# Attention in a two-layer encoder: the transposed softmax weights' 64-row rests of two head groups in one PSUM bank, copied by ScalarE

## The reference, cut to what matters

```python
# 16 query heads, 2 key/value heads of width 64; chunks of 64 frames, window = own chunk + 1 before
scores = einsum("bcqkgd,bcskd->bckgqs", q, k_band) * (HEAD_DIM ** -0.5)
scores = where(valid, scores + bias, NEG_INF)          # bias = -slope[head] * distance
m = maximum(max(scores, axis=-1), sink)
p = exp(scores - m)
denom = sum(p, axis=-1) + exp(sink - m)
o = einsum("bckgqs,bcskd->bcqkgd", p / denom, v_band)
```

## Time and profile before

| | |
|---|---|
| three timed runs | 2421.97, 2423.84, 2426.55 us; median 2423.84 |
| the profiled execution | 2419.16 us, its span 2417.4 us |
| TensorE busy over the span | 2330.7 us (96%) |
| VectorE, ScalarE, GpSimd busy | 1433.3, 793.6, 410.1 us |
| mean granted TensorE clock | 0.987 of full speed |
| attention's rounds | about 1515 to 1649 us of the span |

### The profile page before, as it was taken

One profiled execution on the slowest core, in us unless ns is written; L12 is line 12 of the kernel. 1 busy time (PEld: TensorE's weight loads), 2 busy tenths in 40 slices (PEclk: granted clock), 3 DMA queues, 4 the chain that ended last, 5 costly groups with the idle time before them and its releaser, 6 DMA issues.

```text
span 2417.4 us, 41380 instructions
## 1 busy us (share of the span) xinstructions
PE 2330.7 (96%) x16362; PEld 1900.6 (79%) x16362; DVE 1433.3 (59%) x1994; ACT 793.6 (33%) x1265; POOL 410.1 (17%) x401
## 2 busy tenths in 40 slices
PE   7999989998999999999999999788999999999999
PEld 6888878787778888888888788446788888888887
DVE  4444567775337656755665733873275676567655
ACT  5011234444123322332233423662143233223323
POOL 0000011111322110211121400432311111102110
PEclk9999999999999999999999999998999999999999
DMA  3231100002111111112111110001111111111112
GB/s 126 77 137 57 47 3 4 4 3 98 58 38 53 49 56 52 45 51 61 52 43 52 56 44 27 1 0 44 35 44 54 59 44 51 52 60 44 52 53 88
DMA packets 167185, 119.29 MB, mean 49 GB/s; under 512 B 3663, under 2 KB 164261, under 8 KB 166565
## 3 DMA queue, kind: packets, MB, share of 16 engines
q1 hardware_dynamic: 164284, 100.65, 14.0%
q0 software_dynamic: 2736, 17.04, 1.9%
q10 hardware_dynamic: 56, 0.01, 0.0%
HBM read 106.68 MB, written 10.49 MB: 48 GB/s over the span
## 4 chain that ended last, share of the span: by engine, by line
PE 93%; DVE 5%; issue 1%; ACT 1%; DMA 0%; SPq 0%; DVEq 0%; ACTq 0%
PE ps L280 36%; PE ps L385 25%; PE ps L378 14%; PE ps L1157 2%; PE ps L1179 1%; PE ps L1926 1%; PE ps L2278 1%; PE ps L334 1%; DVE probs L1955 1%; DVE softmax_stats L1960 1%; PE ps L1211 1%; PE ps L1895 1%; PE ps L1690 1%; PE ps L1188 1%; DVE probs_t_b L2009 1%
## 5 line engine op out<-in xcount | busy, mean ns | idle before, releaser
L235 ACT CAST w_hi<-w_raw 128x1024 fp32r<-128x1024 f32 x180 | 189.3, 1052 | 818.1 <-PE ps L280 597.4
L280 PE MATMUL ps<-h_hi,w_hi 128*128 128x512 f32 x1264 | 395.6, 394 | 10.0 <-DVE h_lo L587 6.3
L744 DVE TENSOR_TENSOR residual<-residual,ps 128x512 f32<-128x512 f32 x448 | 299.5, 685 | 159.7 <-PE ps L385 155.8
L280 PE MATMUL ps<-h_lo,w_hi 128*128 128x512 f32 x1264 | 391.5, 391 | 0.0
L280 PE MATMUL ps<-h_hi,w_lo 128*128 128x512 f32 x1264 | 391.5, 391 | 0.0
L280 PEld LDWEIGHTS ps<-h_hi,w_hi 128*128 128x128 f32 x1264 | 236.3, 189 | 60.8 <-issue 10.7
L280 PEld LDWEIGHTS ps<-h_lo,w_hi 128*128 128x128 f32 x1264 | 238.6, 189 | 50.4
L280 PEld LDWEIGHTS ps<-h_hi,w_lo 128*128 128x128 f32 x1264 | 238.6, 189 | 50.2
L239 DVE TENSOR_TENSOR w_lo<-w_raw,w_hi 128x1024 fp32r<-128x1024 f32 x180 | 224.5, 1247 | 25.5 <-ACT w_hi L235 25.5
L712 POOL TENSOR_TENSOR w_sums_raw<-w_raw 128x256 f32<-128x256 f32 x64 | 52.9, 826 | 1079.6 <-DMA w_raw<-in_mlp_down 660.3
L378 PE MATMUL ps<-h_lo,w_hi 128*128 128x512 f32 x512 | 199.2, 389 | 0.0
(11 more groups left out here) (383 smaller groups left out, 3957.3 us busy)
## 6 DMA issues: line engine op xcount, KB each, us to landing
w_raw<-in_mlp_up SPq DMA_DIRECT2D x64, 512.0 KB, 4.0
w_raw<-in_mlp_down SPq DMA_DIRECT2D x64, 512.0 KB, 3.3
w_raw<-in_w_in_ab SPq DMA_DIRECT2D x26, 512.0 KB, 3.8
w_raw<-in_w_qkv SPq DMA_DIRECT2D x10, 512.0 KB, 3.9
x_in_tile<-in_x POOLq DMA_DIRECT2D x8, 512.0 KB, 7.1
x_spill<-residual POOLq DMA_DIRECT2D x1, 4096.0 KB, 12.6
w_raw<-in_w_out_ab SPq DMA_DIRECT2D x8, 512.0 KB, 3.7
w_raw<-in_w_o SPq DMA_DIRECT2D x8, 512.0 KB, 3.8
```

Of the source, the lines that this page charges most:

```text
L235: nc.scalar.copy(WH[:, slot], WR[:, slot]).then_inc(w_hi, 1)
L280: m = nc.tensor.matmul(acc(a_slot, half), ww, xx[:, k, half * HALF:(half + 1) * HALF], start=first, stop=last)
L744: dn_dve.done(TT(xk, xk, PS[:, bank_n, :], ALU.add), step)
```

## The change

The 64-row rests of the values and of the softmax weights are kept in halves of the partitions. The b parts of two groups go to the two halves of bank 5, that of the odd group into rows 64 to 127 by a matmul against the identity in place of a transpose, and ScalarE copies the bank once for both (`r0` behind group 1, `r1` behind group 3). VectorE no longer copies rests. The a parts use banks 4, 6, 7 and 4 for groups 0 to 3. The values exist in a second, shifted token-major form `VREST`, whose 64 rows stand in both halves, made by 8 more transposes and 8 matmuls at the start and copied by ScalarE. The value products go group by group: for each group and each par one product with the 128-row part and one with the 64-row rest, each with 256 moving columns (two heads); output bank 6 takes the even groups and bank 7 the odd ones. They wait for copies group by group.

```diff
-    VTOK = at("v_token_major", [9, P], 190.5)
+    VTOK = at("v_token_major", [NT, P], 190.5)
+    VREST = at("v_rest_twice", [NT, P], 198.5)
-    PTB = at("probs_t_b", [NQ, P], 82)
+    PTB = at("probs_t_b", [NKV, 4, P], 82)
+        def turned(dst, src, half):
+            if half:
+                return nc.tensor.matmul(dst, src, ident, start=True, stop=True)
+            return nc.tensor.transpose(dst, src, ident)
         def v_transposes(t):
...
-            for n in range(9):
-                m = nc.tensor.transpose(bank((6, 7, 5)[n // 4])[:, n % 4], VP[:, P * n:P * n + P], ident)
+            for n in range(NT):
+                m = nc.tensor.transpose(bank(6 + n // 4)[:, n % 4], VP[:, P * n:P * n + P], ident)
+            m.then_inc(v_tr, 1)
+            for n in range(NT):
+                for half in two:
+                    m = turned(bank(4 + n // 4)[half_rows(half), n % 4], VP[:, P * n + P:P * n + P + RH], half)
             m.then_inc(v_tr, 1)
+        def v_rest_act(act):
+            act.wait_ge(v_tr, 2)
+            for n in two:
+                nc.scalar.copy(VREST[:, 4 * n:4 * n + 4], bank(4 + n)).then_inc(v_rest, 1)
...
-            nc.gpsimd.memset(PTB[RH:P], 0.0).then_inc(ptb_zero, 1)
...
-            v_pool.done(nc.gpsimd.tensor_copy(VST[:, s], VTOK[:, bass.ds(tile, 2), :]), "v")
+            for n, (v, step) in enumerate(((VTOK, "own"), (VREST, "rest"))):
+                v_pool.done(nc.gpsimd.tensor_copy(VST[:, s, n], v[:, bass.ds(tile, 1), :]...), step)
...
+        TA_BANK = (4, 6, 7, 4)
         def probs_transposes(t, tile, s, g):
...
-            if g > 0:
-                pv_act.wait(t, tile, f"e{g - 1}")
-                pv_dve.wait(t, tile, f"e{g - 1}")
+            if g == 3:
+                pv_act.wait(t, tile, "e0")
+            elif at_start(tile, 1):
+                t.wait_ge(v_rest, 2)
+            else:
+                pv_act.wait(t, tile - 1, ("r1", "o0", "o1")[g])
+            if g == 2:
+                pv_act.wait(t, tile, "r0")
...
-                m = nc.tensor.transpose(bank(5)[0:RH, j], probs(tile, s, g)[:, j, P:WIN], ident)
+                m = turned(bank(5)[half_rows(g % 2), j], probs(tile, s, g)[:, j, P:WIN], g % 2)
         def value_products(t, tile, s):
...
+            for g in range(4):
+                kv, half = g // 2, g % 2
+                if g < 3:
+                    pv_act.wait(t, tile, ("r0", "e2", "r1")[g])
+                for par in two:
+                    o = PS[half_rows(par), 6 + half].rearrange("p (k a m) -> p k a m", k=NKV, m=P)[:, kv]
+                    nc.tensor.matmul(o, VST[:, s, 0, RH * kv:RH * kv + RH], PTA[:, 4 * g + par:4 * g + 4:2],
+                                     start=True, stop=False, skip_group_check=True)
+                    m = nc.tensor.matmul(o, VST[half_rows(half), s, 1, RH * kv:RH * kv + RH],
+                                         PTB[half_rows(half), kv, par:4:2],
+                                         start=False, stop=True, skip_group_check=True)
+                if g > 1:
+                    pv_pe.done(m, f"pv{half}")
         def round_dve(dve, new, old, s):
...
-                        rest_copy(dve, old, g - 1)
...
-                rest_copy(dve, old, 3)
         def round_act(act, new, old, s):
...
+            if at_start(old, 1):
+                v_rest_act(act)
...
-                    pv_act.done(nc.scalar.copy(PTA[:, 4 * g:4 * g + 4], bank(4)), f"e{g}")
+                    pv_act.done(nc.scalar.copy(PTA[:, 4 * g:4 * g + 4], bank(TA_BANK[g])), f"e{g}")
+                    if g % 2:
+                        pv_pe.wait(act, old, f"tb{g}")
+                        pv_act.done(nc.scalar.copy(PTB[:, g // 2], bank(5)), f"r{g // 2}")
             if old is not None:
-                pv_pe.wait(act, old, "pv")
-                waited(act, "act")
-                for kv in range(NKV):
-                    pv_act.done(nc.scalar.copy(Q[:, 4 * kv:4 * kv + 4, bass.ds(old * P, P)], bank(6 + kv)), f"o{kv}")
+                for half in two:
+                    pv_pe.wait(act, old, f"pv{half}")
+                    waited(act, "act")
+                    pv_act.done(nc.scalar.copy(Q[:, :, bass.ds(old * P, P)]...[:, half], bank(6 + half)...), f"o{half}")
```

More of the change, by code:

```diff
@@ L1817, in v_tokens_dve @@
             dve.wait_ge(v_tr, 1)
-            for n in (0, 1, 2):
-                rows = 4 if n < 2 else 1
-                nc.vector.tensor_copy(VTOK[:, 4 * n:4 * n + rows], bank((6, 7, 5)[n])[:, 0:rows]).then_inc(v_tok, 1)
+            for n in two:
+                nc.vector.tensor_copy(VTOK[:, 4 * n:4 * n + 4], bank(6 + n)).then_inc(v_tok, 1)
+        v_rest = sem("v_rest_token_major")
+        def v_rest_act(act):
+            act.wait_ge(v_tr, 2)
+            for n in two:
+                nc.scalar.copy(VREST[:, 4 * n:4 * n + 4], bank(4 + n)).then_inc(v_rest, 1)
         q_pool = Track("q_tile_copied", ["q"])
-        v_pool = Track("v_tile_copied", ["v"])
+        v_pool = Track("v_tile_copied", ["own", "rest"])
         p_pool = Track("probs_pool", ["p1", "p2", "p3"])
         sc_pe = Track("score_pe", [f"sc{g}" for g in range(4)])
-        pv_pe = Track("value_pe", [f"t{w}{g}" for g in range(4) for w in "ab"] + ["pv"])
+        pv_pe = Track("value_pe", [f"t{w}{g}" for g in range(4) for w in "ab"] + ["pv0", "pv1"])
         sc_dve = Track("score_dve", [f"{w}{g}" for g in range(4) for w in ("b", "max", "neg")] + ["sink"])
-        pv_dve = Track("value_dve", ["den", "rcp", "p0", "e0", "e1", "e2", "e3"])
+        pv_dve = Track("value_dve", ["den", "rcp", "p0"])
         sc_act = Track("score_act", [f"e{g}" for g in range(4)] + ["sink"])
-        pv_act = Track("value_act", [f"e{g}" for g in range(4)] + ["o0", "o1"])
-        ptb_zero, nsnk_ok = sem("probs_rest_zero"), sem("minus_sinks_ready")
+        pv_act = Track("value_act", ["e0", "e1", "r0", "e2", "e3", "r1", "o0", "o1"])
+        nsnk_ok = sem("minus_sinks_ready")
         slopes = [2.0 ** (-8.0 * (h + 1) / NQ) for h in range(NQ)]
@@ L1859, in first_pool @@
             q_tile(pool, 1, 1)
-            q_pool.wait(pool, 1, "q")
-            nc.gpsimd.memset(PTB[RH:P], 0.0).then_inc(ptb_zero, 1)
-            pool.wait_ge(ptb_zero, 1)
         def v_tile(pool, tile, s):
             if not at_start(tile, 2):
-                pv_pe.wait(pool, tile - 2, "pv")
+                pv_pe.wait(pool, tile - 2, "pv1")
                 waited(pool, "pool")
-            v_pool.done(nc.gpsimd.tensor_copy(VST[:, s], VTOK[:, bass.ds(tile, 2), :]), "v")
+            for n, (v, step) in enumerate(((VTOK, "own"), (VREST, "rest"))):
+                v_pool.done(nc.gpsimd.tensor_copy(VST[:, s, n], v[:, bass.ds(tile, 1), :].rearrange("p a n -> p (a n)")),
+                            step)
         def score_products(t, tile, s, g):
@@ L1902, in probs_transposes @@
             else:
-                pv_dve.wait(t, tile, f"p{g}")
-            if g > 0:
-                pv_act.wait(t, tile, f"e{g - 1}")
-                pv_dve.wait(t, tile, f"e{g - 1}")
+                pv_dve.wait(t, tile, "p0")
+            if g == 3:
[6 more added lines that the diff above has]
+                pv_act.wait(t, tile, "r0")
@@ L1907, in probs_transposes @@
             for j in range(4):
-                m = nc.tensor.transpose(bank(4)[:, j], probs(tile, s, g)[:, j, 0:P], ident)
+                m = nc.tensor.transpose(bank(TA_BANK[g])[:, j], probs(tile, s, g)[:, j, 0:P], ident)
             pv_pe.done(m, f"ta{g}")
             for j in range(4):
-                m = nc.tensor.transpose(bank(5)[0:RH, j], probs(tile, s, g)[:, j, P:WIN], ident)
+                m = turned(bank(5)[half_rows(g % 2), j], probs(tile, s, g)[:, j, P:WIN], g % 2)
             pv_pe.done(m, f"tb{g}")
@@ L1928, in value_products @@
-            pv_pe.done(m, "pv")
+            v_pool.wait(t, tile, "rest")
+            for g in range(4):
[11 more added lines that the diff above has]
+                    pv_pe.done(m, f"pv{half}")
@@ L1989, in round_dve @@
                         pv_dve.wait(dve, old, "rcp")
-                    else:
-                        rest_copy(dve, old, g - 1)
                     if g == 0:
@@ L2001, in round_dve @@
                 sc_dve.done(nc.vector.tensor_tensor(STA[:, s, 3], SNK[:, :], STA[:, s, 2], ALU.add), "sink")
-            if old is not None:
-                rest_copy(dve, old, 3)
[L2005 to L2009, removed]
         def round_act(act, new, old, s):
@@ L2026, in round_act @@
                     pv_pe.wait(act, old, f"ta{g}")
-                    pv_act.done(nc.scalar.copy(PTA[:, 4 * g:4 * g + 4], bank(4)), f"e{g}")
+                    pv_act.done(nc.scalar.copy(PTA[:, 4 * g:4 * g + 4], bank(TA_BANK[g])), f"e{g}")
+                    if g % 2:
+                        pv_pe.wait(act, old, f"tb{g}")
+                        pv_act.done(nc.scalar.copy(PTB[:, g // 2], bank(5)), f"r{g // 2}")
             if old is not None:
-                pv_pe.wait(act, old, "pv")
```

(13 more changed lines are left out.)

## The result

The changed kernel takes 2442.74 us (median of 11 runs, 2439.66 to 2448.66), the kernel before 2423.46 (11 runs, 2420.43 to 2437.3). The ratio is **1.0083, interval 1.0067 to 1.0099**: slower by 19.3 us. The forecast was 2439, slower, range 2420 to 2454.

A forecast was written before the change was run, and what follows sets the result against it. TensorE was to become the bound, 18.64 us a round against 16.09. Start +5.8, five rounds +12.8, next -0.1, last -3.1: +15.4 on 2419.16 is 2434.6, in medians 2439 us, range 2420 to 2454.

The forecast's parts named there:

- What bounds the kernel, and what the freed waits give: Attention rounds: VectorE copies stand between TensorE's steps; freed waits give at most about 3 us; TensorE becomes the bound.
- I take it that none run side by side: Value products: sixteen products, one by one at 0.435 us, take 6.96; with changes and tail 8.6 against 3.65.
- A change of form costs 0.10 us: TensorE, where a product's rows-by-columns form changes: 0.10 us each; fifteen changes inside the values, 1.50 us.
- Below that the records' columns exclude it: Value products: 3.65 us is the least they could take, since the records' columns are the same number in all.
- The rest of the round: TensorE outside the value products: four scores 5.16 us and transposes 4.92 in a round of 18.64.
- ScalarE's tightest stretch: From the values' end to `r0`: output copy, two exps, three copies, 6.0 us, covered by TensorE's 6.5.
- The +1.1 for matmuls in place of transposes: Odd groups' rests turned by matmul: +0.55 us each for groups 1 and 3, +1.1 a round at most.
- The start: Up to the first values' end: extra rest transposes, matmuls and form changes, then longer values; 1538.7 against 1532.91, +5.8 us.
- The last rounds: Round without fourth scores 17.35 against 17.46 us, -0.1; last round 15.1 against 18.2, -3.1.
- the halves still overlap: Value products: column halves run as staggered pairs although forms differ; values 3.8 us, launch 2403; chance 0.16.
- Changes that cost nothing: Value products: none side by side but form changes free; values 6.96 us, round 16.8, launch 2423; chance 0.08.
- A clock that falls in the long value stretches: Value products: a 1.2 GHz stretch in each of eight rounds costs 13.6 us more, launch 2453; chance 0.06.

The follow-up runs named there:

- 1 and 2: The runs `halves_in_turn` (2404.0 us) and `one_form` (2394.93 us), each described in its own line.
- experiment 3: Kernel before with its rest products over 64 rows, giving three changes of form inside a round's values; 2429.26 us, one run; the same run as `before_rest_64`.
- rests_four: Changed kernel with a tile's eight own value products first, then its eight rest products, so the form changes once; 2393.44 us, ratio 0.9893 against the kernel before.
- experiment 4: Changed kernel with the odd groups' rests turned by transposes into rows 0 to 63 instead of matmuls (another sum); 2435.44 us, one run.
- halves_in_turn: Changed kernel with each group's value products reordered: both own products, then both rest products, column halves as neighbours; 2404.0 us, ratio 0.9923 against the kernel before.
- one_form: Changed kernel, order unchanged, rest products reading all 128 rows so that all value products have one form (another sum); 2394.93 us, one run.
- before_rest_64: Kernel before with its rest products over 64 rows, otherwise unchanged; 2429.26 us, one run; the same run as experiment 3.

## Why the prediction was right, and where it was not

**What bounds the kernel, and what the freed waits give: right.** It had "about 3 us a round" as the most; the last column gives 2.4. The wait for `probs_t_b` made by VectorE is gone, and TensorE is the bound.

**"I take it that none run side by side": right**, and it decides: the pairs of two records in the timeline, and 1 and 2 show that the form is the reason. The rows that it rested on had 0.07 us of overlap in place of 0.17 where forms changed. The Trainium skill (TensorEngine Tiling (Array Packing), Key Properties) has it that a change of mode drains the engine and tiles of one mode run in parallel; 9.26 us with two forms and 4.05 with one agree with it.

**"A change of form costs 0.10 us": the term that was mis-sized.** Between 128*64 and 64*64 it is 0.15: 0.45 for three in experiment 3, and in the changed kernel a step of 0.575 against 0.435 for its work, 0.14. The prediction took its 0.10 from changes from and to 128*128, and from gaps between rows alone. Against 0.43 for two records of 256 columns the pairs' starts lie 0.575 apart: the gap between rows is some 0.1 of it again, and the rest lies inside the rows, where a gap doesn't show it. Sixteen times 0.04 is 0.64 a round, nearly all of the 0.70 that a round is above the forecast (19.34 against 18.64, values 9.26 against 8.6). By the table the sum of the parts was 3.7 us short (19.1 against 15.4): 3.4 in the five rounds, 0.7 in the next, less 0.4 at the start.

**"Below that the records' columns exclude it": wrong.** The prediction took 3.65 us, two products at a time, as the least that the values could take. `rests_four` takes 3.56 us, its wait for `r1` among it, since four of its 64*64 products run at once. None of the rows that it read shows four at once, and the error didn't bear on the forecast.

**The rest of the round: right in sum, 10.08 forecast and measured, which is luck in part: two errors nearly cancel.** ScalarE's tightest stretch was put at 6.0 us by way of the output copy and called covered by TensorE's 6.5. The one that binds goes through the new scores, VectorE's softmax and exp, 6.84, and TensorE waits 0.25 to 0.3 for it. From the start of the scores in front of that wait to that of the transposes behind it, it is 1.80 us (1569.27 to 1571.07), 0.4 more than the 1.39 of forecast scores and a change. Against this, group 3's matmuls overlap the first own product, 0.49 us from start to start (1573.82 to 1574.31) where group 1's block takes 1.02; the prediction counted one behind the other. The +1.1 for matmuls in place of transposes is there in the rows (L1726 in 1.09, L1727 in 0.60) but is worth nothing by itself (experiment 4).

**The start: +5.4 against +5.8.** The rests' transposes take 4.72 us (4.46 forecast) from the first L1727 at 1520.62 to the scores:

```profile
1519.70 1.09 PE L1734 MATMUL ps<-constants,v_padded 128*128 128x128 f32 x8 [2.20 <-DVE v_padded L623]
...
1525.34 1.56 PE L1911 MATMUL ps<-k_zero_padded,q_tile 128*128 128x384 f32 x4
```

The 0.55 for the low clock at 1513 was not paid in this execution (eight in 1.09 us); in three of the other kernels it was (1.97).

**The last rounds.** -3.1 for the last as forecast, and the round before it +0.6 instead of -0.1, the 0.7 of a middle round again. Both ran at 1.00 where 0.90 and 0.72 had stood, as the sums of the forecast took it; TensorE is busy 17.65 us of 17.90 and 13.77 of 15.30 there.

**The rivals.** That the halves still overlap is wrong: no two pairs are at once in the values' rows. It gave 2403, and `halves_in_turn` takes 2404.0, but that is chance: there the forms still don't overlap, the values take 5.09 us where the rival had 3.8, and a round 15.18 where it had 14.1. Changes that cost nothing: wrong. A clock that falls in the long value stretches: wrong, 1.00 in every round.

## What to carry to other kernels

In these runs products of 64 columns share TensorE's time only with products of the same form at another place. Where a rest has 64 rows, either fill it to the full height with zeros (4.05 us for the block) or put all the products of one form together (3.56), and don't alternate (9.26). Price a change of form by the distance of block starts, not by the gap between rows, and within a form put different places next to each other. A copy taken off a second engine is worth at most the wait that it ends (about 3 us a round here, of which the whole new layout got 2.4); reckon first what the new layout does to the bounding engine.

## What was not expected of the hardware

In these traces matmuls at different places do not start in the order of the program. Group 3's last matmuls (L1726, columns 64 to 127) are issued ahead of the first own product (L1945, columns 0 to 63), and the trace has L1945 starting at 1574.31, L1726 records still at 1574.42. In `one_form` too, the records that share a step start in staggered pairs. The Trainium skill (PSUM — Partial Sum Buffer, Engine vs sequencer instructions) says that matmuls start and complete in program order; of the starts at different places this trace shows the contrary, and the ends are modelled. Within one place and over a change of form the order held.

Transposes into 64 columns follow those into 128 without a gap (L1931 at 1565.55 or 1571.07, L1727 0.44 to 0.49 us after it), while a matmul into columns 64 to 127 of the same 128*64 starts 0.53 after it (1567.72 to 1568.25) and the scores 1.02 after that, a change of form on either side. And four 64*64 places work at once: eight products of 256 columns in 1.02 us (1564.22 to the scores at 1565.24), a change of form included.

Open: why the granted clock fell to 0.50 for 31 us in `before_rest_64` and not for so long in before, and what makes layer 0's clock differ by 0.03 between executions of the same code. Neither was tried. Nor was a version that combines `rests_four` with a cheaper path to `r0`, the next wait by the chain above.
